# Routed experts in which each pass is taken through its down-projection before the next pass's up-projection

## The reference

```python
def moe(h, router_w, router_b, w1, w3, w2):
    t = h.reshape(-1, d)
    ...                                     # scores, best group of 4 experts, best 2 in it, weights
    hid = jax.nn.silu(jnp.einsum('td,edf->tef', t, w1)) * jnp.einsum('td,edf->tef', t, w3)
    hid = hid * combine[:, :, None]
    return jnp.einsum('tef,efd->td', hid, w2).reshape(bsz, s, d)
```

## Time and profile before

| | |
|---|---|
| median of 3 runs | 847.17 us |
| profiled execution, whole | 844.48 us |
| profiled execution, span of the trace | 842.7 us |
| TensorE matmul busy | 670.7 us (80%), 4802 instructions |
| TensorE weight load busy | 344.9 us (41%) |
| VectorE busy | 226.9 us (27%) |
| ScalarE busy | 158.9 us (19%) |
| GpSimd busy | 33.4 us (4%) |
| bytes moved by DMA | 214.72 MB, mean 255 GB/s |
| up matmuls L1537 | 1152, 143.1 us busy |
| down matmuls L1552 | 576, 70.1 us busy |
| chain that ended last | TensorE 66%, DMA 16%, VectorE 8%, issue 7% |

### The profile page before, as it was taken

One profiled execution on the slowest core, in us unless ns is written; L12 is line 12 of the kernel. 1 busy time (PEld: TensorE's weight loads), 2 busy tenths in 40 slices (PEclk: granted clock), 3 DMA queues, 4 the chain that ended last, 5 costly groups with the idle time before them and its releaser, 6 DMA issues.

```text
span 842.7 us, 11378 instructions
## 1 busy us (share of the span) xinstructions
PE 670.7 (80%) x4802; PEld 344.9 (41%) x4802; DVE 226.9 (27%) x552; ACT 158.9 (19%) x313; POOL 33.4 (4%) x80
## 2 busy tenths in 40 slices
PE   4599999989897599979263499999976799792714
PEld 3355555567554533323013344556544233231203
DVE  0404022756125611301000440104247012100015
ACT  3201001443204221101011230300123111110012
POOL 1000000000000110000002000000000000000020
PEclk9899999999999899989598699999988799986857
DMA  9973033079236689999857932233333699999342
GB/s 373 426 335 149 8 150 145 11 294 385 122 150 276 226 341 425 421 430 424 354 234 286 432 146 100 100 150 150 149 150 126 254 423 412 425 429 425 104 174 75
DMA packets 23959, 214.72 MB, mean 255 GB/s; under 512 B 2752, under 2 KB 4576, under 8 KB 12000
## 3 DMA queue, kind: packets, MB, share of 16 engines
q1 hardware_dynamic: 13680, 182.06, 52.4%
q0 software_dynamic: 4320, 15.73, 5.3%
q10 hardware_dynamic: 5904, 16.14, 4.9%
HBM read 199.62 MB, written 14.30 MB: 254 GB/s over the span
## 4 chain that ended last, share of the span: by engine, by line
PE 66%; DMA 16%; DVE 8%; issue 7%; ACT 1%; POOL 1%; SPq 0%; DVEq 0%; ACTq 0%; POOLq 0%
PE bank L1279 26%; PE bank L1537 14%; DMA ring<-in_moe 8%; PE bank L1552 6%; PE bank L1624 5%; DMA ring<-in_ev_in 4%; DVE work L765 2%; DMA work<-y_slots,index 2%; PE bank L1318 2%; DMA y_slots<-work 2%; PE bank L1250 2%; PE bank L1219 2%; PE bank L1411 1%; DVE rstd L791 1%; PE bank L1604 1%
## 5 line engine op out<-in xcount | busy, mean ns | idle before, releaser
L1537 PE MATMUL bank<-ring,work 128*32 128x512 f32 x1152 | 143.1, 641 | 46.8 <-issue 46.8
L1279 PE MATMUL bank<-hT,ring 128*128 128x384 f32 x416 | 137.5, 494 | 3.5 <-DMA ring<-in_ev_in 3.5
L1279 PEld LDWEIGHTS bank<-hT,ring 128*128 128x128 f32 x416 | 80.3, 193 | 60.3 <-DMA ring<-in_ev_in 3.8
L1537 PEld LDWEIGHTS bank<-ring,work 128*32 128x32 f32 x1152 | 38.1, 117 | 136.1 <-issue 136.1
L1279 PE MATMUL bank<-work,ring 128*128 128x384 f32 x256 | 83.3, 487 | 0.3 <-DVE work L765 0.3
L1552 PE MATMUL bank<-ring,work 128*32 128x512 f32 x576 | 70.1, 630 | 10.4 <-DMA ring<-in_moe 10.4
L1279 PEld LDWEIGHTS bank<-work,ring 128*128 128x128 f32 x256 | 48.3, 190 | 34.5 <-DVE work L765 1.3
L1099 DVE COPY work<-bank 128x512 f32<-128x512 f32 x18 | 12.5, 692 | 144.9 <-PE bank L1522 144.9
L1219 PE MATMUL bank<-ring,csil 128*32 128x128 f32 x1024 | 37.6, 309 | 16.3 <-DMA ring<-in_ada_w 16.3
L1624 PE MATMUL bank<-ring,hT 128*128 128x512 f32 x96 | 41.6, 593 | 2.1 <-ACT hT L543 2.1
L529 ACT ACTIVATE sq<-xT 128x384 f32<-128x384 f32 x40 | 20.6, 521 | 115.6 <-DVE xT L768 103.4
(11 more groups left out here) (181 smaller groups left out, 583.7 us busy)
## 6 DMA issues: line engine op xcount, KB each, us to landing
ring<-in_moe SPq DMA_DIRECT2D x32, 2048.0 KB, 15.7
ring<-in_ada_w SPq DMA_DIRECT2D x16, 3072.0 KB, 11.4
ring<-in_moe SPq DMA_DIRECT2D x32, 1024.0 KB, 16.4
ring<-in_ev_in SPq DMA_DIRECT2D x3, 3072.0 KB, 26.5
y_slots<-work ACTq DMA_DIRECT2D x18, 512.0 KB, 10.6
ring<-in_gm_in SPq DMA_DIRECT2D x4, 2048.0 KB, 19.3
ring<-in_ev_out SPq DMA_DIRECT2D x2, 2048.0 KB, 10.2
ring<-in_gm_out SPq DMA_DIRECT2D x2, 2048.0 KB, 7.8
```

Source lines behind the costliest of these rows:

```text
L1279: mm = pe.matmul(ps[:, 0:T], w[:, k, j * P:j * P + P], x[:, k, :], start=(k == 0), stop=(k == KD - 1))
L1537: mm = pe.matmul(bank[p % 2][rows, :], h_slotT[:, p % 2, k * P + BLOCK * n:k * P + BLOCK * n + BLOCK], ring[:, (chunk + e) % SLOTS, k * 51 ...
```

## The change

On TensorE a pass is finished before the next is begun. The order for each pass p is now: turn_h(p+1), transposes of the hidden rows of p, down(p), the whole of up(p+1). ScalarE and VectorE take their steps in the same order: the copy of turn_h(p+1) stands ahead of the copy of the hidden rows of p, and silu and gate of p+1 stand behind the eviction of down(p). The order of the loads on SP, the gathers, the stores, the buffers and all instructions are as before; only places in the queues of three engines change.

```diff
--- before.py
+++ after.py
@@ -638,17 +638,14 @@
                 act.activation(silu[:, p % 2, :], bank[p % 2][:, 0:F], ACT.Silu).then_inc(s_silu[l], 1)
 
             def experts_routed(l):
-                for p in range(2):
-                    copy_h(l, p)
+                copy_h(l, 0)
                 silus(l, 0)
                 for p in range(PASSES):
                     b = p % 2
+                    if p + 1 < PASSES:
+                        copy_h(l, p + 1)
                     act.wait_ge(s_tr[l], p + 1)
                     act.activation(hiddenT[:, b, :], bank[6 + b][:, 0:F], ACT.Identity).then_inc(s_ht[l], 1)
-                    if p + 1 < PASSES:
-                        silus(l, p + 1)
-                    if p + 2 < PASSES:
-                        copy_h(l, p + 2)
                     act.wait_ge(s_expert[l], experts_done(p))
                     if p >= 2:
                         act.wait_ge(s_yst[l][b], 16 * (p // 2))
@@ -656,6 +653,8 @@
                     act.wait_ge(s_y0[l], p + 1)
                     act.wait_ge(s_y1[l], p + 1)
                     act.dma_start(y_slots[p * P:p * P + P, :], y_slot[:, b, :]).then_inc(s_yst[l][b], 16)
+                    if p + 1 < PASSES:
+                        silus(l, p + 1)
 
                 if l == 0:
                     ada(11)
@@ -1104,19 +1103,18 @@
                 tt(hidden[:, p % 2, :], silu[:, p % 2, :], bank[p % 2][:, F:2 * F], ALU.mult).then_inc(s_hid[l], 1)
 
             def experts_routed(l):
-                for p in range(2):
-                    copy_h(l, p)
+                copy_h(l, 0)
                 gate(l, 0)
                 for p in range(PASSES):
                     b = p % 2
-                    if p + 2 < PASSES:
-                        copy_h(l, p + 2)
                     if p + 1 < PASSES:
-                        gate(l, p + 1)
+                        copy_h(l, p + 1)
                     dve.wait_ge(s_expert[l], experts_done(p))
                     if p >= 2:
                         dve.wait_ge(s_yst[l][b], 16 * (p // 2))
                     dve.tensor_copy(y_slot[:, b, 512:D], bank[5][:, :]).then_inc(s_y1[l], 1)
+                    if p + 1 < PASSES:
+                        gate(l, p + 1)
                     if p == 2:
                         index_rows(l)
                 if l == 0:
@@ -1555,26 +1553,22 @@
                     mm.then_inc(s_expert[l], len(finished(p)))
 
                 turn_h(0)
-                up(0, range(KD // 2))
-                turn_h(1)
-                up(0, range(KD // 2, KD))
+                up(0, range(KD))
 
                 for p in range(PASSES):
                     b = p % 2
                     if p + 1 < PASSES:
-                        up(p + 1, range(KD // 2))
+                        turn_h(p + 1)
                     pe.wait_ge(s_hid[l], p + 1)
                     for c in range(2):
                         tr = pe.transpose(bank[6 + b][:, c * P:c * P + P], hidden[:, b, c * P:c * P + P], ident[:, :])
                     tr.then_inc(s_tr[l], 1)
-                    if p + 1 < PASSES:
-                        up(p + 1, range(KD // 2, KD))
-                    if p + 2 < PASSES:
-                        turn_h(p + 2)
                     pe.wait_ge(s_ht[l], p + 1)
                     wait(pe, s_y0[l], p)
                     wait(pe, s_y1[l], p)
                     down(p)
+                    if p + 1 < PASSES:
+                        up(p + 1, range(KD))
 
             def moe(l, excess):
                 n = PRODUCT_AT[("ada_t", 10 if l == 0 else 15)]
```

## The result

The changed kernel takes 841.37 us (median of 5 runs, 838.32 to 843.04) against 847.17 (844.02 to 847.69). The ratio is 0.9943, 95% interval 0.9918 to 0.9968: faster, by 5 to 6 us, or 0.6%. The forecast was 831 us, faster by 16. The direction was right, the size was not: about a third of the gain came.

A forecast was written before the change was run, and what follows sets the result against it. Expert stages were taken as DMA-bound up to 778 (layer 1), then a serial tail. Gains of 8.4 us in layer 1 and 7.6 in layer 0 sum to -16.0, from 847.2 to 831; range 824 to 843.

The forecast's parts named there:

- What bounds the kernel: Expert stages: DMA-bound as far as 778 in layer 1, then a 26 us serial tail with hardly any transfers.
- the first rival: Expert stages: the queue never runs dry and no down weights are late; -24.7 us, giving 822.5; chance 0.12.
- The pass: A pass on TensorE without weight waits costs 12.56 us, 0.6 more than now.
- the walk: Layer 1 loads and passes timed in order: down(8) ends at 795.6, 8.4 us earlier; layer 0 taken as 7.6 us.
- the start, costed at nothing: Stage start: turn_h(1), gather 3, U3 and expert-number reads come 3.6 us later; costed at nothing, 2 us if dry.
- Part 3: The weight loads of the expert stages, said to decide; holds the start's cost and the walk; sum -16.0 us.
- the four signs of being wrong: Passes 0 to 2 over 13 us, clock falling in them, down(3) not waiting, or U15 landing later than 790.
- The other late term: D5 and pass 4: Layer 1: down(3) waits 5.3 us for D5; only after up(4) do U9, U10, D8 enter a dry queue.
- the tail's gain: Stage end, in the first rival: down(8) ends 13.1 us earlier in layer 1, 11.6 in layer 0, together 24.7.
- the starvation rival: Passes 4 to 7: down(p) waits for the queue's end, later up loads are freed too late; about 844; chance 0.15.
- The rival of the clock: Gap between up and down drops the clock every pass: 17.4 us passes, 11.8 us later each layer, 871; chance 0.09.
- the fixed cost of a load: A load issued into a dry queue has 3.1 us added fixed time, where the skill page gives about 2.0.

The follow-up runs named there:

- swap of pass 7 alone: Kernel before with only down(7) put ahead of up(8), silu and gate of pass 8 behind the evictions of pass 7: 824.3 us, ratio 0.9743.
- the one with the old start: Changed kernel with turn_h(1) put back between the halves of up(0): 836.22 us, ratio 0.9895.
- (alone): Kernel before with only turn_h(1) moved behind all of up(0): 850.51 us against 845.31, ratio 1.0064.
- the runs with U3 let go: Changed kernel with U3 no longer waiting for gather 3: 836.86 us, ratio 0.9888; the same on the swap of pass 7 alone: 822.78 us.
- leaving pass 3 out: Old start, down(p) ahead of up(p+1) in every pass but pass 3, turn_h(p+2) in each pass: 827.17 us, ratio 0.9781 to the kernel before.
- with the waits of the down-projections taken away: Changed kernel with SP issuing, for each pass, the freed down loads before the up loads: 841.84 us, ratio 0.9965 to the kernel before.

## Why the prediction was wrong

**What bounds the kernel.** Right. The stage is DMA-bound as far as U15, and a serial tail follows. The swap of pass 7 alone is this finding made into a kernel; it gave 20.6 us where the first rival, a queue that never runs dry, had 24.7. One reading was too wide: outside the expert stages the DMA does not always move less, since slices 1 and 22 have 426 and 432 GB/s.

**The pass.** Right: 12.38 us in place of 12.56, and 11.97 before. The new waits came at down(3), down(5), down(6) and down(7), as in the walk, with 8.98, 5.67, 3.44 and 2.96 us, the handoff of 0.47 in each, for 5.3, 3.6, 2.3 and 4.8 without it. up(8) to down(8) took 9.07 us for 9.1.

**The step that failed: the start, costed at nothing.** Part 3 says "The queue still holds work then, and I cost this at nothing; if it ran dry there, 2 us". It ran dry. The 3.6 us of the delay were themselves too few. up(0) now waits for both copies of turn_h, which puts it 0.9 us later, and its matmuls take 0.6 us more than counted by the slow clock they begin at, so U3 was 5.1 us late. The queue of loads held no more than U2 and D2, 3 MB, sent from 662.80 on. U3 was sent only at 673.80, and from 673 to 676 the DMA moved 123, 102 and 258 GB/s where it had moved 410 the us before. By the runs the start costs 4.6 us (changed kernel against the one with the old start) and 5.2 (alone). A layer that is 2.3 to 2.6 us, near the 2 us named for a dry queue; what failed is the premise that the queue would still hold work. It is the cost that I set at zero, and the runs with U3 let go show that it goes by way of SP: a step moved on TensorE delays a gather, by that the load behind it, by that 12 register reads, and by that U4. I had named these and not followed them with numbers. None of the four signs of being wrong that the prediction lists came (U15 landed at 789.2, with the limit at 790), because none of them looked at the start.

**The other late term: D5 and pass 4.** This was in the walk: down(3) waits, U9 goes out late, the queue is dry near 725. The forecast priced it through the difference of the walk (831) to the first rival (822.5), 8.5 us. Measured by leaving pass 3 out: 836.2 - 827.2 = 9.0 us. This size was right, though the 8.5 was to cover all that the other passes cost too.

**The account.** From the kernels in the table, each against the next: the tail's swap -20.6 us; swaps of passes 0, 1, 2, 4, 5 and 6 +2.9; the swap of pass 3 +9.0; the late start +4.6. The sum is -4.1, the measured difference of 840.8 and 844.9. It closes by its form, since these are neighbours in one chain of kernels; each difference is measured, with some 3 us of uncertainty. (Between the kernel with the old start and the one without pass 3, turn_h also stands one pass earlier; that part was not tried by itself.) Set beside the forecast, which is -24.7 and 8.5 with rounding, the same four terms are the miss of 12 us: the start 4.6 for nothing, the tail's gain 4.1 too large, the other swaps 2.9 for nothing of their own, pass 3 0.5 more. (Against the first result, 841.4, the miss is 10 us, because the kernel before was 2.3 us slower there.) Only the start, at 4.6 and 5.2 us in two pairs of kernels, is clear of the scatter; for the tail and the other swaps the share is not shown.

The traces say the same of the kernel with the old start, 836.2 against 831. Its stages end at 140.5 and 141.1, where the walk, with 0.8 us to the store, has 139.1 and 140.0: 2.5 us in the two. Part of that is down(6), whose wait I had priced without the slow clock (in layer 1 it took 5.02 us for 3.46): it holds up up(7), by that the issue of U15, and up(8) waits 1.28 us for it. Outside the stages the profiled execution took 551.2 us and that of the kernel before 549.4, and its median is 3.4 us above it, where I had 2.7. That these last 2.5 us are more than scatter is not shown: runs of the kernel before cover 840.28 to 850.02 us.

**The rivals.** The measured time lies where the starvation rival had its range (840 to 847), and so inside the stated 824 to 843, but that is luck, for its mechanism did not happen. It asked for dry spells in each of the passes 4 to 7, and there was one of any length there, plus one at the very start that no rival had. The rival of the clock fell: the granted clock stayed at 1.00 in the passes without a wait (696 to 706). The rule of the Trainium skill on back-to-back matmuls ("Perfetto Trace Analysis", section "Matmul Optimizations") therefore decided nothing between the passes; it shows in the down-projections after a wait, at 5.3 to 6.5 us for 3.46, as priced, and in up(0). For the fixed cost of a load the trace again has more than the 2.0 us that the Trainium skill gives in "DMA: Bandwidth & Descriptors", section "Anatomy of one DMA — SWDGE (gpsimd) path", for transfers issued by GpSimd, while these are issued by SP: U9, issued into the empty queue at 731.68, landed after 8.1 us, and 8.1 - 4.95 is 3.1.

**The better version.** Pass 7 alone, at 824.3 us, beats both kernels. With U3 not paced it came to 822.78 (ratio 0.9718, interval 0.9677 to 0.9759):

> The swap of pass 7 alone, with U3 not waiting for gather 3. The queue starts its unbroken stretch earlier by what it now idles between U2 and U3, if it idles at all. Theory B (the bytes bound the stage from U2 on): no idle time there in the kernel before, so within 2 us of the swap of pass 7 alone. If the register reads, which stand behind U3, bound the start: up to 4 us a layer less.

The intervals of the two overlap, so a gain of 1 or 2 us is not shown. It agrees with theory B, within 2 us of pass 7 alone: the queue had no empty time to win there.

## What to carry to other kernels

Where a stage is bound by its loads, swap the order of work first where the engine stands idle for the last of them. There the swap frees a buffer during a wait that is there anyway; elsewhere it may hold up the step that frees the next large buffer, as it did in pass 3 and not in the passes 4 to 6. Follow each moved step to the queue that issues loads, through every semaphore on the way, and write down when the bytes still queued will have landed; a few us of an empty queue were not made up in this stage, which is bound by bytes. That a wait stands before some instruction says little: with the waits of the down-projections taken away (21.1 us), the same time stood before the up-projections (21.6 us).

## What was not expected of the hardware

The clock after short gaps. In the changed kernel's layer 0, down(8) came 1.18 us after the two transposes, which themselves had 0.95 us of idle time before them, and it ran at the slow clock:

```profile
435.07 0.44 PE L1564 MATMUL bank<-smalls,work 128*128 128x128 f32 x2 [0.95 <-DVE work L764]
436.69 5.34 PE L1550 MATMUL bank<-ring,work 128*32 128x512 f32 x32 [1.18 <-DMA ring<-in_moe]
```

In layer 1 the same place had 0.95 and 0.61 us, and down(8) took 3.64 us; in the kernel with pass 7 alone it had 0.96 and 1.41 us and took 5.27. In the earlier trace rows one gap of 1.24 us cost nothing. So 0.57 us less of waiting went with 1.7 us less for the same matmuls, and the length of one gap alone does not tell whether it costs: the one that cost nothing had dense work before it, the others only two transposes after another gap. Nor does dense work before decide it. In the kernel without pass 3 down(4) of layer 1 had down(3), turn_h and the transposes before it without a gap and lost nothing after 2.95 us. In the kernel with the old start down(7) had up(7), turn_h and the transposes before it without a gap and took 5.34 us after 2.67. The line of the former:

```profile
714.40 3.64 PE L1558 MATMUL bank<-ring,work 128*32 128x512 f32 x32 [2.95 <-DMA ring<-in_moe]
```

What tells these cases apart is open. Also, stages of one kernel differ by up to 3 us between two executions, which is more than most of the effects here; so the medians and the chain of neighbouring kernels carry the argument.
